# First modulation's second half in two quarters, and k blocks 4 to 7 of the first four tiles in two passes

## The chip, the cores and the metric

One NeuronCore of a Trainium2 chip runs the whole kernel as one program. The metric is the device time of one execution in microseconds; lower is better. The program drives five engines, each with its own instruction stream: TensorE (PE, with its weight loads as PEld), VectorE (DVE), ScalarE (ACT), GpSimd (POOL) and SyncE (SP), which here only issues DMAs. Streams meet through counting semaphores.

## The reference

A decoder layer on 512 tokens of width 1024, in float32: a token mixer, then a mixture of experts, then a final norm. The change lies in the very start, where the conditioning vector `c` is turned into a shift and a scale and applied to the normed input, and in the first columns of the input projection:

```python
mod = silu(c) @ w_ada + b_ada            # w_ada: 1024 x 6144
sh1, sc1, g1, sh2, sc2, g2 = split(mod, 6)
h = rmsnorm(x, norm_mix_g) * (1 + sc1) + sh1
proj = h @ w_in                          # w_in: 1024 x 7168
```

Only `sh1` and `sc1` (columns 0 to 1023 and 1024 to 2047 of `w_ada`) are needed for `h`. The kernel holds `h` transposed, channels on the partitions, as eight blocks `k` of 128 channels by 512 tokens.

## The kernel before

**Precision.** A float32 product is made of three matmuls: `h` and the weights are each split into a high part and the rest (`h_hi`, `h_lo`, `w_hi`, `w_lo`), and `mm3` (lines 571 to 573) issues hi by hi, hi by lo and lo by hi. One output tile (128 columns of `w_in` by 512 tokens) takes 8 blocks `k` of three matmuls, 24 in all.

**Weight chunks.** `w_in` comes in chunks of 256 columns (1 MB), two tiles each. SyncE loads chunk n into `w_raw[n % 2]`; ScalarE makes `w_hi` of it (`split_hi`, L952) and VectorE `w_lo` (`split_lo`, L1203). Both targets have two slots, so `split_hi(n)` waits until the last tile of chunk n-2 is done (`chunk_used`), and tile 2n may not start on TensorE until `split_lo(n)` has ended (`pe.wait_ge(s_lo, n + 1)`, L749). Chunks 0 and 1 are split in halves by k (`half_hi`, `half_lo`: blocks 0 to 3, then 4 to 7).

**Modulation.** The columns of `w_ada` come in eight pieces of 1 MB, two (k halves) for each of four groups `b` of 512 columns: b = 0 and 1 are the first 512 columns of shift and of scale, b = 2 and 3 their second 512. `ada_rows(b, h)` multiplies a piece with `silu(c)` (four small matmuls, each of which shows as two in the profile, so L585 x16 is both halves), `ada_out(b)` copies the sums out (ScalarE, L956), `ada_columns(b)` transposes them into columns (TensorE, L598). VectorE's `mod_columns(g)` then makes shift and scale of four blocks `k` at once: it waits for both groups of its half (`s_acp` at 2g + 2). After that `h_scale(k)` (VectorE, L1238), `h_high(k)` (ScalarE, L961) and `h_low(k)` (VectorE, L1244) make block k of `h`.

**The first four tiles** lie in four PSUM banks, since their first four blocks `k` are multiplied before the modulation of the other four is known. TensorE's order, written out by hand, is: blocks 0 to 3 of tiles 0 and 1; rows of b = 2; blocks 0 to 3 of tile 2; rows of b = 3 and columns of b = 2; blocks 0 to 3 of tile 3 with the columns of b = 3 inside; then blocks 4 to 7 of tiles 0 and 1, k by k in turn; then of tile 2; then of tile 3. From tile 4 on a loop over the steps runs tile after tile. On ScalarE the order after this is: copy out tiles 0 and 1 (L989), `split_hi(2)`, copy out tiles 2 and 3, `split_hi(3)`.

The order on SyncE is: the two halves of `x`, the pieces of b = 0 and 1, chunks 0 and 1, the pieces of b = 2 and 3, the masks, then chunk 2 once `w_lo` of chunk 0 is done.

Of the kernel before, what the change touches and what calls it, by code (L numbers as in the profile page):

```python
# [30 lines left out]
ALU = mybir.AluOpType  # L31
AX = mybir.AxisListType

P = 128
T = 512
D = 1024
KT = D // P
# [11 lines left out]
CHW = 256  # L49
# [16 lines left out]
C_C, C_BADA, C_GMIX, C_LB, C_ON = 0, 8, 24, 32, 40  # L66
# [27 lines left out]
def trunk_kernel(nc, xT, x, cols, consts, masks, w_ada, b_ada_row, w_in, w_o_hgrn, w_o_conv,  # L94
# [15 lines left out]
    with ctx:  # L110
# [10 lines left out]
        def at(name, where, shape, dt=F32, plus=0):  # L121
            return nc.alloc_sbuf_tensor_at(name, shape, dt, offset=placed[where] + plus)
# [27 lines left out]
        for l in range(1, NLEV + 1):  # L150
# [9 lines left out]
        ada_w = [at(f"ada_w{i}", r, [P, 4, T]) for i, r in  # L160
                 enumerate(("F", "K", "Q", "V", "TOT", "OG", "DG", "ST"))]
# [13 lines left out]
        cols_t = at("cols_t", "COLS", [P, C_ALL])  # L175
# [6 lines left out]
        mod1 = at("mod1", "SMALL", [P, 16])  # L182
# [13 lines left out]
        ada_s = at("ada_s", "SMALL", [P, 8], F32, 352)  # L196
# [27 lines left out]
        pp = ctx.enter_context(nc.psum_tensor("pp", [P, 1024], F32))  # L224
# [15 lines left out]
        s_ada = [sem(f"ada_piece{i}_loaded") for i in range(8)]  # L240
        s_raw = [sem(f"raw_chunk_loaded{i}") for i in range(2)]
        s_hi = sem("chunk_hi_done")
        s_lo = sem("chunk_lo_done")
# [13 lines left out]
        s_acp = sem("ada_columns_pe")  # L257
        s_md = sem("ada_columns_done")
# [4 lines left out]
        s_hl = sem("h_lo_done")  # L263
# [82 lines left out]
        s_as = sem("ada_columns_summed")  # L346
# [23 lines left out]
        def bank_of(s):  # L370
            return ha[:, s - 2, :] if s in (2, 3) else proj[:, s % 2, :]
# [71 lines left out]
        def chunk_view(ap, n):  # L443
            return ap[:, n % 2, :].rearrange("p (k n) -> p k n", k=4 if chunks[n][0] == "yb" else 8)
# [21 lines left out]
        def _(sp):  # L466
# [3 lines left out]
            wa = w_ada[0].rearrange("(k p) n -> p k n", p=P)  # L470

            def ada_first(b):
                for h in range(2):
                    i, c0 = 2 * b + h, D * (b % 2) + T * (b // 2)
                    sp.dma_start(ada_w[i][:, :, :], wa[:, 4 * h:4 * h + 4, c0:c0 + T]).then_inc(s_ada[i], 16)  # L475

            def chunk_load(n):
                sp.dma_start(chunk_view(w_raw, n), chunk_source(n)).then_inc(s_raw[n % 2], 16)
# [1 line left out]
            for h in range(2):  # L480
                sp.dma_start(xt_t[:, 4 * h:4 * h + 4, :], xTv[:, 4 * h:4 * h + 4, :]).then_inc(s_xt[h], 16)
            ada_first(0)
            ada_first(1)
            chunk_load(0)
            chunk_load(1)
# [82 lines left out]
        def _(pe):  # L568
            def mm3(outap, a_hi, a_lo, b_hi, b_lo, first, last):

                pe.matmul(outap, a_hi, b_hi, start=first, stop=False)  # L571
                pe.matmul(outap, a_hi, b_lo, start=False, stop=False)  # L572
                return pe.matmul(outap, a_lo, b_hi, start=False, stop=last)  # L573
# [6 lines left out]
            pe.wait_ge(s_par, 16 * 2)  # L580

            def ada_rows(b, h):
                pe.wait_ge(s_ada[2 * b + h], 16)
                for j in range(4):
                    mm = pe.matmul(ha[32 * j:32 * j + 32, b, :], cact32[:, 4 * h + j, :], ada_w[2 * b + h][:, j, :],  # L585
                                   start=(h == 0), stop=(h == 1))
                if h:
                    mm.then_inc(s_ao, 1)

            def ada_columns(b):  # L590
                pe.wait_ge(s_ac, b + 1)
                if b == 0:
                    pe.wait_ge(s_sq0, 1)
                elif b >= 2:
                    pe.wait_ge(s_md, 2)
                for c in range(4):
                    q = 512 * (b % 2) + P * c
                    mm = pe.transpose(pp[:, q:q + P], ada_r[:, b, P * c:P * c + P], ident)  # L598
                mm.then_inc(s_acp, 1)

            def first_part(s, k):
                n, t = steps[s][2], steps[s][3]
                hi, lo = chunk_view(w_hi, n), chunk_view(w_lo, n)
                mm = mm3(bank_of(s), hi[:, k, P * t:P * t + P], lo[:, k, P * t:P * t + P],
                         h_hi[:, k, :], h_lo[:, k, :], k == 0, k == KT - 1)
                if k == KT - 1:
                    mm.then_inc(s_tile, 1)
# [18 lines left out]
            pe.wait_ge(s_lf, 2)  # L626
            for k in range(4):
                first_part(2, k)
            ada_rows(3, 0)
            ada_rows(3, 1)  # L630
            ada_columns(2)
            for k in range(4):
                first_part(3, k)
                if k == 1:
                    ada_columns(3)
            pe.wait_ge(s_lo, 1)
            for k in range(4, KT):
                pe.wait_ge(s_hl, k + 1)
                first_part(0, k)
                first_part(1, k)  # L640
            pe.wait_ge(s_lo, 2)
            for s in (2, 3):
                for k in range(4, KT):
                    first_part(s, k)

            def level(qd, l):
# [283 lines left out]
        def raw_ready(eng, n):  # L930
            eng.wait_ge(s_raw[n % 2], 16 * (n // 2 + 1))

        @block.scalar
        def _(act):
# [19 lines left out]
            def ada_out(b):  # L954
                act.wait_ge(s_ao, b + 1)
                act.activation(ada_r[:, b, :], ha[:, b, :], ACT.Copy).then_inc(s_ac, 1)  # L956

            def h_high(k):
                act.wait_ge(s_md, 2 * (k // 4) + 2)
                act.wait_ge(s_ht, k + 1)  # L960
                act.activation(h_hi[:, k, :], xt_t[:, k, :], ACT.Identity, bias=mod1[:, k:k + 1]).then_inc(s_hh, 1)  # L961

            def half_hi(n, half):
                raw_ready(act, n)
                part_ = slice(1024 * half, 1024 * half + 1024)
                act.activation(w_hi[:, n, part_], w_raw[:, n, part_], ACT.Copy).then_inc(s_hi if half else s_hf, 1)
# [11 lines left out]
            half_hi(0, 1)  # L978
            half_hi(1, 1)
            ada_out(2)  # L980
            ada_out(3)
            for k in range(4, KT):
                h_high(k)

            def evacuate(s, kind, tile, n, t):
                bank = bank_of(s)
# [185 lines left out]
        def _(dve):  # L1172
# [47 lines left out]
            def mod_columns(g):  # L1220

                dve.wait_ge(s_acp, 2 * g + 2)
                dve.tensor_reduce(ada_s[:, :], pp[:, :].rearrange("p (q j r) -> p q j r", j=4, r=32)[:, :, :, 0], AX.X,
                                  ALU.add).then_inc(s_as, 1)
                dve.wait_ge(s_as, g + 1)
                dve.tensor_tensor(mod1[:, :].rearrange("p (a k) -> p a k", a=2)[:, :, 4 * g:4 * g + 4],
                                  ada_s[:, :].rearrange("p (a k) -> p a k", a=2),
                                  cols_t[:, C_BADA:C_BADA + 16].rearrange("p (a k) -> p a k", a=2)[:, :, 4 * g:4 * g + 4],
                                  ALU.add).then_inc(s_md, 1)
                dve.wait_ge(s_md, 2 * g + 1)  # L1230
                dve.scalar_tensor_tensor(mod1[:, 8 + 4 * g:12 + 4 * g], mod1[:, 8 + 4 * g:12 + 4 * g], 1.0,
                                         cols_t[:, C_GMIX + 4 * g:C_GMIX + 4 * g + 4],
                                         ALU.add, ALU.mult).then_inc(s_md, 1)

            def h_scale(k):
                dve.wait_ge(s_md, 2 * (k // 4) + 2)
                dve.wait_ge(s_rdone, 1)
                dve.scalar_tensor_tensor(xt_t[:, k, :], xt_t[:, k, :], mod1[:, 8 + k:9 + k], rst[:, :],  # L1238
                                         ALU.mult, ALU.mult).then_inc(s_ht, 1)

            def h_low(k):
                dve.wait_ge(s_ht, k + 1)
                dve.wait_ge(s_hh, k + 1)
                dve.scalar_tensor_tensor(h_lo[:, k, :], xt_t[:, k, :], mod1[:, k:k + 1], h_hi[:, k, :].bitcast(F32),  # L1244
                                         ALU.add, ALU.subtract).then_inc(s_hl, 1)

            def half_lo(n, half):
                dve.wait_ge(s_hi if half else s_hf, n + 1)
                raw_ready(dve, n)
                part_ = slice(1024 * half, 1024 * half + 1024)  # L1250
                dve.tensor_tensor(w_lo[:, n, part_], w_raw[:, n, part_], w_hi[:, n, part_].bitcast(F32),
                                  ALU.subtract).then_inc(s_lo if half else s_lf, 1)

            for g in range(2):
                mod_columns(g)
                h_scale(4 * g)
                if g == 0:
                    half_lo(0, 0)
                for k in range(4 * g + 1, 4 * g + 4):
                    h_scale(k)  # L1260
                    h_low(k - 1)
                h_low(4 * g + 3)
                if g == 0:
                    half_lo(1, 0)
                    half_lo(0, 1)
                    half_lo(1, 1)

            def evacuate(s, kind, tile, n, t):
                bank = bank_of(s)
# [487 lines left out]
            for tt in range(TT + 1):  # L1757
# [7 lines left out]
                if tt:  # L1765
                    q = tt - 1
# [154 lines left out]
```

## Time and profile before

| what | value |
|---|---|
| median of 3 runs | 866.62 us (866.6, 866.62, 869.02) |
| the profiled execution's own time | 867.63 us |
| its span, first to last instruction | 865.8 us |
| mean granted TensorE clock | 0.984 |
| PE, DVE, ACT busy | 93%, 55%, 24% of the span |
| instructions | 14136 |

Times in the trace count from the span's start. A row of the timeline gives start and duration in microseconds, engine, line, operation, output and inputs; a bracket gives the idle time of that engine before it and who ended it. The ends of matmuls are modelled, so successive matmuls overlap in the rows: the step from one start to the next is the rate. The granted clock is the share of full speed (2.4 GHz) that TensorE was given: 1.00 or 0.50 (1.2 GHz).

### The profile page before, as it was taken

How to read it: one execution, taken by the hardware profiler on the slowest of the kernel's cores; microseconds unless marked ns; L12 is line 12 of the kernel's file. 1: busy time of each engine (PE TensorE's matmuls, PEld its weight loads, DVE VectorE, ACT ScalarE, POOL GpSimd, SP SyncE). 2: the span in 40 equal slices, each digit the busy share in tenths (PEclk: the TensorE clock that was granted, in tenths of full speed). 3: DMA queues.
4: the chain of work that ended last, by engine and by line, in shares of the span. 5: the costliest groups of instructions: out<-in, count | busy, mean ns of one | idle time of the engine just before them, and what ended most of it. 6: DMA issues, size and time to landing. Idle time of an engine off the chain costs nothing.

```text
span 865.8 us, 14136 instructions
## 1 busy us (share of the span) xinstructions
PE 805.5 (93%) x5706; PEld 585.9 (68%) x5706; DVE 476.3 (55%) x644; ACT 205.0 (24%) x263; POOL 143.5 (17%) x199
## 2 busy tenths in 40 slices
PE   2899999999999999999999999989999999999960
PEld 0578889888789887778888898655555555555520
DVE  2648999996799964878777465611111111111117
ACT  3441221222331126522222423100000000000012
POOL 0000231221413200320000000012222222222220
PEclk9999999999999999999999999999999999999995
DMA  9923231313131311278774949997999999998316
GB/s 311 370 81 103 98 98 50 98 50 97 50 98 51 98 49 49 98 246 280 240 241 160 341 142 388 401 381 289 378 395 395 400 390 400 394 396 303 125 43 274
DMA packets 102207, 191.59 MB, mean 221 GB/s; under 512 B 4151, under 2 KB 41287, under 8 KB 102161
## 3 DMA queue, kind: packets, MB, share of 16 engines
q1 hardware_dynamic: 89042, 160.79, 51.4%
q10 hardware_dynamic: 9168, 19.40, 6.6%
q0 software_dynamic: 3952, 10.76, 3.4%
q8 instruction: 33, 0.54, 0.3%
q14 instruction: 12, 0.10, 0.0%
HBM read 182.54 MB, written 10.49 MB: 223 GB/s over the span
## 4 chain that ended last, share of the span: by engine, by line
PE 82%; DVE 9%; DMA 3%; issue 2%; SPq 1%; ACT 1%; POOL 1%; DVEq 0%; POOLq 0%; ACTq 0%
PE proj L869 19%; PE proj L571 14%; PE proj L573 14%; PE proj L572 14%; PE ha L905 10%; PE pp L678 2%; DMA w_raw<-in_w_in 2%; PE pp L859 2%; DVE acc L1366 1%; SPq L475 1%; PE ha L891 1%; PE ha L708 1%; PE ha L741 1%; DVE rt L1540 1%; PE ha L711 1%
## 5 line engine op out<-in xcount | busy, mean ns | idle before, releaser
L869 PE MATMUL proj<-ew,heT 128*64 128x256 f32 x1536 | 175.0, 381 | 0.7 <-ACT heT L1142 0.7
L869 PEld LDWEIGHTS proj<-ew,heT 128*64 128x64 f32 x1536 | 107.9, 137 | 66.2 <-issue 16.4
L571 PE MATMUL proj<-h_hi,w_hi 128*128 128x512 f32 x368 | 146.8, 399 | 3.8 <-DVE h_lo L1244 3.2
L573 PE MATMUL proj<-h_hi,w_lo 128*128 128x512 f32 x368 | 144.1, 392 | 0.0
L572 PE MATMUL proj<-h_lo,w_hi 128*128 128x512 f32 x368 | 143.9, 391 | 0.0
L1203 DVE TENSOR_TENSOR w_lo<-w_raw,w_hi 128x2048 fp32r<-128x2048 f32 x36 | 82.4, 2289 | 20.4 <-ACT w_hi L952 20.3
L1366 DVE SCALAR_TENSOR_TENSOR acc<-u_t,cols_t,acc 128x512 f32<-128x512 f32 x120 | 91.1, 807 | 0.6
L905 PE MATMUL ha<-ew,aT 128*64 128x512 f32 x384 | 87.7, 598 | 0.9 <-DVE aT L1732 0.9
L571 PEld LDWEIGHTS proj<-h_hi,w_hi 128*128 128x128 f32 x368 | 69.5, 189 | 21.9 <-issue 7.6
L952 ACT ACTIVATE w_hi<-w_raw 128x2048 fp32r<-128x2048 f32 x36 | 68.7, 1908 | 65.8 <-PE proj L573 43.1
L572 PEld LDWEIGHTS proj<-h_lo,w_hi 128*128 128x128 f32 x368 | 69.6, 189 | 14.4 <-issue 0.5
L573 PEld LDWEIGHTS proj<-h_hi,w_lo 128*128 128x128 f32 x368 | 69.4, 189 | 14.7
L1737 DVE TENSOR_TENSOR y_sb<-ha,rows 128x512 f32<-128x512 f32 x24 | 16.6, 691 | 90.9 <-PE ha L905 90.9
L1831 POOL COPY gi<-idx_g 128x1 int32 (+1 forms) x25 | 4.7, 188 | 318.4 <-DVE idx_g L1715 185.2
L905 PEld LDWEIGHTS ha<-ew,aT 128*64 128x64 f32 x384 | 25.5, 136 | 46.1 <-issue 45.8
L1726 DVE TENSOR_TENSOR a_t<-proj,sg_t 128x256 f32<-128x256 f32 x24 | 10.2, 426 | 77.7 <-PE proj L869 77.7
L1732 DVE COPY aT<-ha 128x256 f32<-128x256 f32 x24 | 10.2, 425 | 74.0 <-PE ha L891 74.0
L1482 DVE SCALAR_TENSOR_TENSOR ada_acc<-ada_p,cact,ada_acc 128x512 f32<-128x512 f32 x64 | 47.9, 751 | 3.0 <-DMA ada_p<-in_w_ada 1.1
L1136 ACT ACTIVATE sg_t<-proj 128x256 f32<-128x256 f32 x24 | 9.2, 383 | 150.3 <-PE proj L869 150.3
L1142 ACT ACTIVATE heT<-pp 128x512 f32<-128x512 f32 x25 | 14.9, 597 | 102.1 <-PE pp L859 102.1
L571 PE MATMUL proj<-w_hi,m_hi 128*128 128x256 f32 x128 | 37.0, 289 | 0.0
L571 PE MATMUL proj<-w_hi,h_hi 128*128 128x256 f32 x128 | 36.8, 288 | 0.0
(254 smaller groups left out, 1211.7 us busy)
## 6 DMA issues: line engine op xcount, KB each, us to landing
ew<-in_w_gate SPq DMA_DIRECT2D x32, 1024.0 KB, 13.8
ew<-in_w_up SPq DMA_DIRECT2D x32, 1024.0 KB, 15.1
ew<-in_w_down SPq DMA_DIRECT2D x32, 1024.0 KB, 14.4
w_raw<-in_w_in SPq DMA_DIRECT2D x28, 1024.0 KB, 5.2
ada_p<-in_w_ada ACTq DMA_DIRECT2D x16, 1024.0 KB, 5.3
ada_w<-in_w_ada SPq DMA_DIRECT2D x8, 1024.0 KB, 13.8
w_raw<-in_w_o_hgrn SPq DMA_DIRECT2D x4, 1024.0 KB, 6.0
w_raw<-in_w_out SPq DMA_DIRECT2D x4, 1024.0 KB, 10.0
```

Of the source, the lines that this page charges most:

```text
L571: pe.matmul(outap, a_hi, b_hi, start=first, stop=False)
L572: pe.matmul(outap, a_hi, b_lo, start=False, stop=False)
L573: return pe.matmul(outap, a_lo, b_hi, start=False, stop=last)
L678: mm = pe.matmul(pp[64 * j:64 * j + keys, 32 * u:32 * u + 32], k_t[:, h, t0:t0 + keys], tblk(q_t[:, h, t0:t0 + 64], m, 1), start=True, sto ...
L859: mm = pe.transpose(pp[:, P * c:P * c + P], xg[:, P * c:P * c + P], ident)
L869: mm = pe.matmul(out_ps[JS * i:JS * i + JS, 0:FG], heT[:, c_, JS * j_:JS * j_ + JS], w[:, k, FG * i:FG * i + FG], start=(kb == 0), stop=(k ...
L905: mm = pe.matmul(ha[JS * i:JS * i + JS, 1, 0:DG_], aT[:, c_, JS * i_:JS * i_ + JS], w[:, k, DG_ * i:DG_ * i + DG_], start=(fb == 0), stop= ...
L952: act.activation(w_hi[:, n % 2, :], w_raw[:, n % 2, :], ACT.Copy).then_inc(s_hi, 1)
L1203: dve.tensor_tensor(w_lo[:, n % 2, :], w_raw[:, n % 2, :], w_hi[:, n % 2, :].bitcast(F32), ALU.subtract).then_inc(s_lo, 1)
L1366: dve.scalar_tensor_tensor(acc[:, ct, :], src, tap, acc[:, ct, :], ALU.mult, ALU.add).then_inc(s_cv, 1)
L1482: dve.scalar_tensor_tensor(dst, ada_p[g % 2][:, k, :], cact[:, kk:kk + 1], dst, ALU.mult, ALU.add).then_inc(s_aa, 1)
L1737: dve.tensor_tensor(y_sb[:, :], ha[:, 1, 0:DG_], rows[:, 3, 0:DG_], ALU.mult).then_inc(s_y, 1)
```

## The change

The pieces of b = 2 and 3 are cut another way. Each now holds 256 columns of shift and the 256 columns of scale that belong to the same two blocks: b = 2 is the modulation of blocks 4 and 5, b = 3 that of blocks 6 and 7. Each piece comes in two DMAs of 512 KB with rows of 1 KB, where it was one DMA of 1 MB with rows of 2 KB. VectorE computes each quarter by itself (`mod_quarter`) as soon as its one group of columns is there. TensorE's order becomes: rows of b = 2; tile 2's blocks 0 to 3 with the columns of b = 2 after block 1; tile 3's; rows of b = 3; blocks 4 and 5 of tile 0; columns of b = 3; blocks 4 and 5 of tile 1, 2, 3; then blocks 6 and 7 of tiles 0, 1, 2, 3. ScalarE makes `h_hi` of blocks 4 and 5 before it copies out the rows of b = 3.

```diff
--- before.py
+++ after.py
@@ -471,8 +471,13 @@
 
             def ada_first(b):
                 for h in range(2):
-                    i, c0 = 2 * b + h, D * (b % 2) + T * (b // 2)
-                    sp.dma_start(ada_w[i][:, :, :], wa[:, 4 * h:4 * h + 4, c0:c0 + T]).then_inc(s_ada[i], 16)
+                    i, ks = 2 * b + h, slice(4 * h, 4 * h + 4)
+                    if b < 2:
+                        sp.dma_start(ada_w[i][:, :, :], wa[:, ks, D * b:D * b + T]).then_inc(s_ada[i], 16)
+                    else:
+                        for a in range(2):
+                            sp.dma_start(ada_w[i][:, :, CHW * a:CHW * a + CHW],
+                                         wa[:, ks, D * a + CHW * b:D * a + CHW * b + CHW]).then_inc(s_ada[i], 16)
 
             def chunk_load(n):
                 sp.dma_start(chunk_view(w_raw, n), chunk_source(n)).then_inc(s_raw[n % 2], 16)
@@ -580,7 +585,7 @@
             pe.wait_ge(s_par, 16 * 2)
 
             def ada_rows(b, h):
-                pe.wait_ge(s_ada[2 * b + h], 16)
+                pe.wait_ge(s_ada[2 * b + h], 32 if b >= 2 else 16)
                 for j in range(4):
                     mm = pe.matmul(ha[32 * j:32 * j + 32, b, :], cact32[:, 4 * h + j, :], ada_w[2 * b + h][:, j, :],
                                    start=(h == 0), stop=(h == 1))
@@ -626,21 +631,26 @@
             pe.wait_ge(s_lf, 2)
             for k in range(4):
                 first_part(2, k)
+                if k == 1:
+                    ada_columns(2)
+            for k in range(4):
+                first_part(3, k)
             ada_rows(3, 0)
             ada_rows(3, 1)
-            ada_columns(2)
-            for k in range(4):
-                first_part(3, k)
-                if k == 1:
+            pe.wait_ge(s_lo, 1)
+            for s in (0, 1):
+                for k in (4, 5):
+                    pe.wait_ge(s_hl, k + 1)
+                    first_part(s, k)
+                if s == 0:
                     ada_columns(3)
-            pe.wait_ge(s_lo, 1)
-            for k in range(4, KT):
-                pe.wait_ge(s_hl, k + 1)
-                first_part(0, k)
-                first_part(1, k)
             pe.wait_ge(s_lo, 2)
             for s in (2, 3):
-                for k in range(4, KT):
+                for k in (4, 5):
+                    first_part(s, k)
+            for s in range(4):
+                for k in (6, 7):
+                    pe.wait_ge(s_hl, k + 1)
                     first_part(s, k)
 
             def level(qd, l):
@@ -956,7 +966,7 @@
                 act.activation(ada_r[:, b, :], ha[:, b, :], ACT.Copy).then_inc(s_ac, 1)
 
             def h_high(k):
-                act.wait_ge(s_md, 2 * (k // 4) + 2)
+                act.wait_ge(s_md, (2, 2, 4, 6)[k // 2])
                 act.wait_ge(s_ht, k + 1)
                 act.activation(h_hi[:, k, :], xt_t[:, k, :], ACT.Identity, bias=mod1[:, k:k + 1]).then_inc(s_hh, 1)
 
@@ -978,9 +988,11 @@
             half_hi(0, 1)
             half_hi(1, 1)
             ada_out(2)
+            h_high(4)
+            h_high(5)
             ada_out(3)
-            for k in range(4, KT):
-                h_high(k)
+            h_high(6)
+            h_high(7)
 
             def evacuate(s, kind, tile, n, t):
                 bank = bank_of(s)
@@ -1233,7 +1245,7 @@
                                          ALU.add, ALU.mult).then_inc(s_md, 1)
 
             def h_scale(k):
-                dve.wait_ge(s_md, 2 * (k // 4) + 2)
+                dve.wait_ge(s_md, (2, 2, 4, 6)[k // 2])
                 dve.wait_ge(s_rdone, 1)
                 dve.scalar_tensor_tensor(xt_t[:, k, :], xt_t[:, k, :], mod1[:, 8 + k:9 + k], rst[:, :],
                                          ALU.mult, ALU.mult).then_inc(s_ht, 1)
@@ -1251,19 +1263,38 @@
                 dve.tensor_tensor(w_lo[:, n, part_], w_raw[:, n, part_], w_hi[:, n, part_].bitcast(F32),
                                   ALU.subtract).then_inc(s_lo if half else s_lf, 1)
 
-            for g in range(2):
-                mod_columns(g)
-                h_scale(4 * g)
-                if g == 0:
-                    half_lo(0, 0)
-                for k in range(4 * g + 1, 4 * g + 4):
-                    h_scale(k)
-                    h_low(k - 1)
-                h_low(4 * g + 3)
-                if g == 0:
-                    half_lo(1, 0)
-                    half_lo(0, 1)
-                    half_lo(1, 1)
+            def mod_quarter(b):
+
+                ks = slice(2 * b, 2 * b + 2)
+                dve.wait_ge(s_acp, b + 1)
+                dve.tensor_reduce(ada_s[:, 0:4], pp[:, 512 * (b % 2):512 * (b % 2) + 512].rearrange("p (q j r) -> p q j r", j=4, r=32)[:, :, :, 0],
+                                  AX.X, ALU.add).then_inc(s_as, 1)
+                dve.wait_ge(s_as, b)
+                dve.tensor_tensor(mod1[:, :].rearrange("p (a k) -> p a k", a=2)[:, :, ks],
+                                  ada_s[:, 0:4].rearrange("p (a k) -> p a k", a=2),
+                                  cols_t[:, C_BADA:C_BADA + 16].rearrange("p (a k) -> p a k", a=2)[:, :, ks],
+                                  ALU.add).then_inc(s_md, 1)
+                dve.wait_ge(s_md, 2 * b - 1)
+                dve.scalar_tensor_tensor(mod1[:, 8 + 2 * b:10 + 2 * b], mod1[:, 8 + 2 * b:10 + 2 * b], 1.0,
+                                         cols_t[:, C_GMIX + 2 * b:C_GMIX + 2 * b + 2],
+                                         ALU.add, ALU.mult).then_inc(s_md, 1)
+
+            mod_columns(0)
+            h_scale(0)
+            half_lo(0, 0)
+            for k in range(1, 4):
+                h_scale(k)
+                h_low(k - 1)
+            h_low(3)
+            half_lo(1, 0)
+            half_lo(0, 1)
+            half_lo(1, 1)
+            for b in (2, 3):
+                mod_quarter(b)
+                h_scale(2 * b)
+                h_scale(2 * b + 1)
+                h_low(2 * b)
+                h_low(2 * b + 1)
 
             def evacuate(s, kind, tile, n, t):
                 bank = bank_of(s)
```

## Rows read from the trace of the kernel before

**Rows 1.** The page: busy time by engine, and the chain that ended last, by engine.

```profile
PE 805.5 (93%) x5706; PEld 585.9 (68%) x5706; DVE 476.3 (55%) x644; ACT 205.0 (24%) x263; POOL 143.5 (17%) x199
...
PE 82%; DVE 9%; DMA 3%; issue 2%; SPq 1%; ACT 1%; POOL 1%; DVEq 0%; POOLq 0%; ACTq 0%
```

**Rows 2.** Timeline of TensorE, 38 to 61.4 and 373 us (start, duration, operation, idle).

```profile
38.17 0.50 PE L571 MATMUL ha<-h_hi,w_hi 128*128 128x512 f32 x1
...
46.50 0.40 PE L573 MATMUL ha<-h_hi,w_lo 128*128 128x512 f32 x1
...
48.73 0.47 PE L571 MATMUL proj<-h_hi,w_hi 128*128 128x512 f32 x1 [1.84 <-DVE h_lo L1244]
...
55.66 0.39 PE L573 MATMUL proj<-h_hi,w_lo 128*128 128x512 f32 x1
55.89 0.39 PE L571 MATMUL ha<-h_hi,w_hi 128*128 128x512 f32 x1
...
61.33 0.39 PE L571 MATMUL proj<-h_hi,w_hi 128*128 128x512 f32 x1
...
372.91 0.50 PE L571 MATMUL proj<-cs_hi,w_hi 128*128 128x512 f32 x1 [1.72 <-DVE mb L1309]
```

**Rows 3.** Windows: busy time and count by engine, granted clock, DMA share, GB/s.

```profile
46.90:48.70 1.80, 0.00 (x0) 0.00 (x0) 1.54 (x4) 1.39 (x2) 0.00 (x0) 1.00 0.03 9
50.50:52.30 1.80, 1.80 (x6) 1.33 (x5) 1.49 (x3) 0.72 (x1) 0.00 (x0) 0.50 0.00 0
360.00:380.00 20.00, 16.24 (x69) 12.48 (x68) 15.27 (x20) 4.31 (x6) 11.33 (x5) 1.00 0.41 134
```

**Rows 4.** Timeline, the small matmuls and copies of the second half's modulation.

```profile
36.32 1.92 PE L585 MATMUL ha<-ada_w,cact 128*32 128x512 f32 x16
...
41.16 1.92 PE L585 MATMUL ha<-ada_w,cact 128*32 128x512 f32 x16
...
43.15 0.60 ACT L956 ACTIVATE ada_r<-ha 128x512 f32<-128x512 f32 x1 [4.24 <-PE ha L585]
...
44.90 0.60 PE L598 MATMUL pp<-con_t,ada_r 128*128 128x128 f32 x4
```

**Rows 5.** Timeline of VectorE and ScalarE from the modulation to `h_lo` of block 4.

```profile
45.54 0.19 DVE L1223 TENSOR_REDUCE ada_s<-pp 128x8 f32<-128x32 f32 x1 [7.69 <-PE pp L598]
...
46.16 1.42 DVE L1238 SCALAR_TENSOR_TENSOR xt_t<-xt_t,mod,rst 128x512 f32<-128x512 f32 x2
...
47.83 0.75 DVE L1244 SCALAR_TENSOR_TENSOR h_lo<-xt_t,mod,h_hi 128x512 fp32r<-128x512 f32 x1 [0.26 <-ACT h_hi L961]
```

**Rows 6.** Timeline of the split of weight chunk 2, after tiles 0 and 1.

```profile
55.41 1.28 ACT L989 ACTIVATE acc<-proj 128x512 f32<-128x512 f32 x2 [4.02 <-PE proj L573]
...
56.58 1.91 ACT L952 ACTIVATE w_hi<-w_raw 128x2048 fp32r<-128x2048 f32 x1
...
58.52 2.29 DVE L1203 TENSOR_TENSOR w_lo<-w_raw,w_hi 128x2048 fp32r<-128x2048 f32 x1 [6.28 <-ACT w_hi L952]
```

**Rows 7.** Windows: 24 to 26 us moves rows of 1 KB, 32 to 34 rows of 2 KB.

```profile
24.00:26.00 2.00, 1.28 (x11) 0.37 (x11) 0.72 (x1) 0.60 (x1) 0.00 (x0) 1.00 1.10 348
32.00:34.00 2.00, 2.00 (x11) 1.66 (x10) 1.74 (x3) 1.40 (x3) 0.00 (x0) 1.00 1.06 389
```

**Rows 8.** SyncE's DMA issues by timeline, and by the DMA view their landing.

```profile
20.54 3.53 SPq L475 DMA_DIRECT2D ada_w<-in_w_ada  x1
...
24.11 2.93 SPq L475 DMA_DIRECT2D ada_w<-in_w_ada  x2
27.08 1.81 SPq L475 DMA_DIRECT2D ada_w<-in_w_ada  x1
...
ada_w<-in_w_ada SPq DMA_DIRECT2D x2, 1024.0 KB, 11.6
ada_w<-in_w_ada SPq DMA_DIRECT2D x1, 1024.0 KB, 14.6
...
w_raw<-in_w_in SPq DMA_DIRECT2D x2, 1024.0 KB, 9.4
```

## The prediction

> **What bounds the kernel now.** I read the page first: TensorE is busy 93% of the span and 82% of the chain that ended last is TensorE's [rows 1]. So a change that moves no TensorE work can gain only where TensorE stands still or runs at the lower clock. I then listed TensorE's idle times in the timeline. Between the first projection matmul and 107 us there is one: after the matmul at 46.50 nothing runs until 48.73, 1.84 us by the bracket, ended by `h_lo` [rows 2]. This is the wait for the second half's modulation. The windows show a second loss beside it: through the gap the granted clock is 1.00, and from 50.5 to 52.3 it is 0.50 [rows 3], the lower level of 1.2 GHz. It fell just after TensorE had stood still. Its price: the 24 matmuls of tiles 0 and 1 from 48.73 to 55.89 took 7.16 us, the 24 of tiles 2 and 3 from 55.89 to 61.33 took 5.44 us, a pitch of 0.227 [rows 2]. So the fall cost 1.72 us. Together the wait and the fall are worth 3.7 us at most: the step from 46.50 to 48.73 is 2.23, less a pitch 2.0, plus 1.7.
>
> Third, because the wait lies ahead of a fixed piece of work, I asked what limits the next thing, tile 4 at 61.33. It needs `w_lo` of weight chunk 2, whose target slot is free only when tile 1 is done. The rows give that chain [rows 2, 6]: tile 1's last matmul at 55.66 ends at 56.05; ScalarE copies out tile 1 (its two copies run 55.41 to 56.69), then makes `w_hi` 56.58 to 58.49; VectorE makes `w_lo` 58.52 to 60.81. From 56.05 to 60.81 is 4.76 us. TensorE started tile 4 at 61.33 without a wait, so the slack is about 0.4 us, and only because tiles 2 and 3 put 24 matmuls, 5.4 us, behind tile 1.
>
> **The change part by part.** *The wait in front of blocks 4 to 7.* TensorE's work up to the last pass is unchanged in count: 24 matmuls, the rows of b = 3 and two sets of columns lie between 38.17 and 46.73 (the start at 46.50 plus a pitch), 8.56 us [rows 2]. The new order puts between them 24 more, blocks 4 and 5 of all four tiles, 5.45 us. If nothing waits, the last pass (blocks 6, 7) starts at 38.17 + 8.56 + 5.45 = 52.18.
>
> Does anything wait? Blocks 4, 5: tile 2's first six matmuls end at 38.17 + 1.4 = 39.6, the columns take 0.6 [rows 4], `h_lo` of block 4 ended 48.58 - 44.90 = 3.7 us after the columns began and block 5's about 0.7 later [rows 4, 5]. So they are ready at about 43.3 and 44.0. TensorE wants them after tiles 2 and 3 (5.45), the columns (0.4) and the rows of b = 3 (1.9): 38.17 + 7.8 = 46.0. Slack 2 us. Blocks 6, 7: rows of b = 3 end at about 46.0, their copy takes 0.6 and starts 2.0 after the rows began [rows 4], so it is out at 46.7, before block 5 of tile 0 is through (46.0 + 1.4 = 47.4). The columns start there; 3.7 us later, and here a little more since both scales go before the first `h_low` (0.7 at most, which is one of them), block 6 is ready at 51.1 to 51.8 against 52.18, and block 7 0.7 later against its use 0.7 later. No wait; the slack is only 0.4 to 1.1. So this wait goes: 2.0 us, and the fall of the clock at this place with it.
>
> *VectorE and SyncE.* `mod_quarter` twice instead of `mod_columns` once adds three small operations, 0.6 us by their steps from 45.54 to 46.16 [rows 5]. They lie in VectorE's idle time (7.69 us ahead of 45.54), so nothing. Uncovered they would cost 0.6. SyncE issues four more DMAs. A bound from below is nothing, since SyncE's next work waits for `w_lo` of chunk 0; from above 4 x 3.5, the longest issue of a piece [rows 8]: the pieces would be issued by 28.9 + 14 = 42.9, the masks and chunk 2 (36.7 before) by about 46, and chunk 2, which took 9.4 to land, would be there at 55, when `w_hi` first needs it (below). I take nothing: half of each piece is half an issue, and the slack is 9 us.
>
> *Rows of 1 KB.* Where the weight chunks' 1 KB rows move, the rate is 348 GB/s, against 389 with the pieces' 2 KB rows [rows 7]: 3.01 against 2.70 us for 1 MB. The first pair of pieces, issued at 20.54 and 24.11 with 11.6 us in the median, lands at about 32.6 and 35.3; with 0.3 us more each the second lands at 35.9. TensorE wants it at 36.32 [rows 4]: covered, by 0.4. The last piece, issued at 27.08 plus 14.6 = 41.7, lands at about 42.9, and is wanted at 44.1 now, since tile 3 goes first. So nothing, with 0 and 2.4 as ends: 2.4 if the second piece takes the slowest landing of its kind, 14.6 instead of about 11.2, and lands at 38.7. I take nothing, since the rate's own rows put it at 35.9. The Trainium skill, DMA: Bandwidth & Descriptors, section Specifications, has 512 B as the least size for line rate, so by it the 1 KB rows would cost nothing; the 348 against 389 of this trace do not agree, and the measured pair decides. The same page (Bandwidth, Measured) asks for transfers of at least 1 MiB, and the change halves them; that is the fourth rival's direction.
>
> *What is late next.* Tile 1 now ends after the first 12 matmuls of the last pass: its last matmul starts at 52.18 + 12 x 0.227 - 0.23 = 54.68, ends at 55.07, and 4.76 us later, at 59.83, `w_lo` of chunk 2 is done. From the end of `h_lo` (47.83 + 0.75) to the matmul it released was 0.15 [rows 2, 5], so tile 4 starts at 59.98. Behind tile 1 there are only the 12 matmuls of tiles 2 and 3: they are through at 52.18 + 24 x 0.227 = 57.63. So TensorE waits from 57.8 (end of the last) to 59.98, 2.2 us, in a place where it did not wait before. Queued behind it on TensorE is everything: tile 4 and the whole projection. Tile 4 moves from 61.33 to 59.98: -1.35 us.
>
> *The clock again.* The new gap is longer than the one that goes. What idle time lets the clock fall here is bounded by rows: 1.84 us was followed by a fall [rows 2, 3]; 1.72 us before 372.91 was not, since all of 360 to 380 has 1.00 [rows 2, 3]. 2.2 us is beyond both, so I take a fall, at the measured 1.72. Ends: 0 and 1.72. Then tile 4's work is through as if it had started at 61.70: +0.37 against the profiled execution.
>
> **The sum, and against what.** Profiled: wait -2.0, clock there -1.7, new wait +2.3 (59.98 - 57.63), clock here +1.7: +0.3 to +0.4. From 867.63 that is 868.0. The median of the runs is 866.62, 1.0 below the profiled execution; I do not know whether the clock fell in those runs too. If it falls in both or in neither, the difference is the same +0.35, since without a fall the kernel before starts tile 4 at 61.33 - 1.72 = 59.61. I put the forecast on the median: 867.0. Behind tile 4 TensorE's chain runs on without a large wait, so a shift is carried to the end as it is. About 0.3% (2.6 us) is what a measurement of this kernel tells from no change.
>
> **The rivals.** (1) *The clock holds in the new gap* while it fell at the old one. For it: the 1.7 us that kept the clock. Against: 2.2 is more than 1.84. Time: 866.62 - 1.35 = 865.3. (2) *Slower: the clock falls in the new gap, and in the runs of before it did not at the old one.* It is decided by where the limit lies, between 1.72 and 1.84 us of standing still by the rows, so the old gap is right at it and the new one past it; that the median lies 1.0 us below the profiled execution, where it did fall, speaks for it, that a profile may cost time by itself against. Time: 59.98 + 1.72 - 59.61 = +2.1, 868.7. (3) *The whole 3.7 comes home*, the split of chunk 2 being hidden anyway. It would need `split_hi(2)` ahead of tile 1's end, which `chunk_used` forbids, or a copy and split chain of 2.5 us where the rows have 4.76. Time: 862.9. (4) *The halved transfers land late* and the second piece holds TensorE at 36.3. It decides once 2 MB after 29.9 (35.3 less two times 2.70) need more than 6.4 us, below 328 GB/s, where the rows have 348. Price up to 2.4; with half of that on top of the forecast, 868.2.
>
> **How the numbers follow.** Forecast 45%, (1) 23%, (2) 17%, (3) 8%, (4) 7%. The range 864.7 to 868.8 holds the forecast and (1), (2), (4) but for their edges, and leaves (3) out. The likeliest case by itself is 866.5 to 867.6. Faster by more than 0.3% (below 864.0) is (3) and an edge of (1): 11%. Slower by more than 0.3% (above 869.2) is (2) and (4) coming together or running over: 9%. Within: 80%.
>
> **What would show it.** The wait ahead of tile 0's block 4 is gone, and blocks 6, 7 start near 52.2 with no idle before them. A new idle time of about 2.2 us stands before tile 4's first matmul, ended by `w_lo` L1203, whose own wait is for `w_hi` L952. The windows after it show a granted clock under 1.00 (forecast, 2) or 1.00 (1). `ada_rows` of b = 2 still starts near 36.3; if later, (4). I am wrong if tile 4 starts without a wait, if a wait for `h_lo` remains in front of block 6, or if a part of the shift at tile 4 is not found at the end.

## The result, and the profile after

The changed kernel takes 870.03 us in the median of 14 runs (867.38 to 872.39), the kernel before 867.31 in 14 runs beside it (866.06 to 871.18). The ratio is 1.0027, 95% interval 1.0015 to 1.0040: slower by 0.3%. A second comparison on another occasion (e8 below) gave 1.0014, 0.9998 to 1.0029. The forecast was 867.0 in 864.7 to 868.8, so the measured time lies outside the range, above it. The profiled execution took 870.24, its span 868.4. Two executions in the later comparisons, one of e5 (1052 us) and one of the kernel before beside it (4633 us), were disturbed and are left out of the numbers.

The page has the same engines busy as before [rows 1]; TensorE's busy time is 2.5 us longer with the same 5706 matmuls, which is a first sign of a lower clock rather than of more work:

```profile
PE 808.0 (93%) x5706; PEld 586.6 (68%) x5706; DVE 476.7 (55%) x647; ACT 204.9 (24%) x263; POOL 143.3 (17%) x199
```

The timeline of the stretch from block 4 to tile 4, to be read against [rows 2, 5, 6]:

```profile
46.73 0.50 PE L576 MATMUL proj<-h_hi,w_hi 128*128 128x512 f32 x1
...
52.79 0.39 PE L576 MATMUL proj<-h_hi,w_hi 128*128 128x512 f32 x1
...
55.28 0.39 PE L578 MATMUL proj<-h_hi,w_lo 128*128 128x512 f32 x1
...
55.70 0.60 ACT L1001 ACTIVATE acc<-proj 128x512 f32<-128x512 f32 x1 [0.76 <-PE proj L578]
...
56.20 1.91 ACT L962 ACTIVATE w_hi<-w_raw 128x2048 fp32r<-128x2048 f32 x1
...
58.14 2.29 DVE L1215 TENSOR_TENSOR w_lo<-w_raw,w_hi 128x2048 fp32r<-128x2048 f32 x1 [5.26 <-ACT w_hi L962]
...
60.49 0.50 PE L576 MATMUL proj<-h_hi,w_hi 128*128 128x512 f32 x1 [2.10 <-DVE w_lo L1215]
```

No idle time stands before blocks 4 (46.73) and 6 (52.79). The last pass starts 21.58 us after the first projection matmul (31.21), where the forecast had 52.18 - 30.70 = 21.48; the wait went as forecast. In its place TensorE stands still for 2.10 us ahead of tile 4, ended by `w_lo` of chunk 2: the chain of [rows 6], 4.76 us from the end of tile 1 to the end of `w_lo`, is unchanged (55.67 to 60.43), and there are only 12 matmuls to cover it. The rows of b = 2 start at 36.86, 5.65 us after the first projection matmul, against 5.62 before, so the halved transfers held nothing up. The windows show what came after this gap, and a second place of the same kind (busy time by engine, granted clock, DMA share, GB/s):

```profile
61.60:64.80 3.20, 3.20 (x9) 2.52 (x8) 1.60 (x1) 0.00 (x0) 0.00 (x0) 0.50 0.98 314
...
566.70:570.00 3.30, 3.01 (x14) 1.71 (x16) 0.00 (x0) 0.24 (x1) 1.12 (x2) 0.50 1.04 377
```

The third column from the right is the granted clock. It fell to 0.50 (1.2 GHz) behind tile 4's gap, and again at 566 us, just behind TensorE's wait for the second gather of tokens for the experts:

```profile
565.65 0.66 PE L869 MATMUL pp<-con_t,xg 128*128 128x128 f32 x4 [2.08 <-DMA xg<-h_rows,gi]
```

In the profile before, that gather had an idle time of 1.80 us and no fall.

The two profiled executions can be compared stretch by stretch. In the one before, a group of small matmuls of the token mixer (L678) and the last group of matmuls of the kernel start at

```profile
257.51 2.06 PE L678 MATMUL pp<-q_t,k_t 128*64 128x32 f32 x64 [0.74 <-DVE st L1377]
...
834.19 3.65 PE L905 MATMUL ha<-ew,aT 128*64 128x512 f32 x16 [0.93 <-DVE aT L1732]
```

and in the one after at

```profile
258.37 2.06 PE L688 MATMUL pp<-q_t,k_t 128*64 128x32 f32 x64 [0.73 <-DVE st L1408]
...
836.83 3.65 PE L915 MATMUL ha<-ew,aT 128*64 128x512 f32 x16 [0.93 <-DVE aT L1763]
```

The first projection matmul starts 0.51 us later (31.21 against 30.70). From there to the first of these rows the change costs 0.35 us (227.16 against 226.81), the forecast's number, with a fall of the clock in each. The later stretch costs 1.78 us more than before (578.46 against 576.68), and it is the one with the gather: its tokens are there 0.29 us later, counted from the group before them, and the fall behind it takes the rest, 1.5 us. The three add up to the 2.6 us between the spans.

**A tool for what follows.** Each run is recorded with its mean granted clock. Each of the 14 profiles has one fall at the very end, when TensorE has finished. In the eight that have no other, the mean is 0.985 to 0.987; in the four with one more it is 0.983 or 0.984, in the two with two more 0.981 or 0.982. One fall costs 1.7 us of 866, or 0.002; so 0.984 or less is read as at least one fall while TensorE still had work. The fall at the end starts between 838 and 843 us, which by itself moves the mean by as much as 0.002, so 0.985 does not exclude a fall, and the mean does not say where one was. By this reading all 14 runs of the changed kernel have at least one.

### The profile page after: what moved, and what is told of

It is laid out like the page before. It is cut to its first block, busy times and chain, and to the rows that moved or that the text cites. A ratio compares the mean times of both kernels' runs of the same rounds, so it can differ in the third digit from the quotient of the medians.

```text
span 868.4 us, 14143 instructions
## 1 busy us (share of the span) xinstructions
PE 808.0 (93%) x5706; PEld 586.6 (68%) x5706; DVE 476.7 (55%) x647; ACT 204.9 (24%) x263; POOL 143.3 (17%) x199
## 4 chain that ended last, share of the span: by engine, by line
PE 83%; DVE 9%; DMA 3%; issue 2%; ACT 2%; POOL 1%; SPq 0%; POOLq 0%; DVEq 0%; ACTq 0%
PE proj L879 19%; PE proj L576 14%; PE proj L578 14%; PE proj L577 14%; PE ha L915 10%; PE pp L688 2%; PE pp L869 2%; DVE acc L1397 1%; DMA xt_t<-in_xT 1%; PE ha L901 1%; PE ha L590 1%; PE ha L718 1%; PE ha L751 1%; DVE w_lo L1215 1%; DVE rt L1571 1%
```

## The experiments

Theory after the result: the work is as forecast and the loss is the clock, which falls more often in the new gap than in the old one. Rivals: the 1 KB loads delay the start; the new order costs time by itself; the 2.7 us are chance.

**e1.** TensorE is kept running through the new gap, with matmuls whose result nobody reads.

```diff
+                if s == 4:
+                    busy(ha[:, 3, :], 8)
                 if t == 0:
                     pe.wait_ge(s_lo, n + 1)
```

> The changed kernel with 8 throw-away 128x128 matmuls in the idle time ahead of tile 4 (2.10 us idle in its profile, one such matmul takes 0.24 us). Clock theory: what the change loses is the fall of the clock in that gap; with TensorE kept running the clock stays at 1.00 there, tile 4 still starts near 60.5, and the time is 1.7 us below the changed kernel's 870.0, so about 868.3, within 0.1% of the kernel before. Rival, the 1 KB loads or the new order itself: the clock is held but the time stays near 870.

867.94 us (12 runs), ratio to the kernel before 0.9998 (0.9981 to 1.0015). Tile 4 starts where it did in the timeline, and the clock is whole behind it:

```profile
60.48 0.50 PE L576 MATMUL proj<-h_hi,w_hi 128*128 128x512 f32 x1 [0.32 <-DVE w_lo L1217]
```

and in the windows (busy time by engine, granted clock, DMA share, GB/s):

```profile
61.00:65.00 4.00, 4.00 (x19) 3.28 (x19) 2.19 (x1) 0.00 (x0) 0.00 (x0) 1.00 0.86 280
```

Eight matmuls that do nothing take about 2 us off the changed kernel's time (its ratios are 1.0027 and, in e8, 1.0014, measured on other occasions), though tile 4 starts no earlier. So the rivals, which have the loss elsewhere, fall for the larger part. In 7 of the 12 runs the mean clock is still 0.984 or less.

**e2.** The same in the kernel before, ahead of block 4: `busy(ha[:, 3, :], 7)`.

> The kernel before with 7 throw-away 128x128 matmuls in its 1.84 us wait ahead of tile 0's block 4. Clock theory: if the clock fell there in all runs, the time drops by 1.7 us to about 865.6; if in only some of them, by that part of 1.7 (half: 866.5); if only in the profiled one, by nothing. The profile shows 1.00 all through the first 110 us. Rival (the fall is no cost, TensorE has slack behind it): no change in time though the clock holds.

868.32 us, ratio 0.9996 (0.9980 to 1.0013). A miss: no gain. The gap is filled (block 4 at 48.46, idle 0.28) and the clock whole behind it (1.00 from 49 to 53 us), but in 8 of 12 runs the mean clock is still 0.984 or less, against 18 of the 35 runs of the unfilled kernel beside them, and the one profile says where:

```profile
563.64 0.55 PE L860 MATMUL pp<-con_t,xg 128*128 128x128 f32 x3 [2.79 <-DMA xg<-h_rows,gi]
```

and in the windows (busy time by engine, granted clock, DMA share, GB/s):

```profile
565.80:569.00 3.20, 3.20 (x18) 1.84 (x17) 0.00 (x0) 0.00 (x0) 0.30 (x1) 0.54 1.04 388
```

The gather is a second place where the clock may fall, in either kernel, and has to be filled too before small differences can be read. What is missing in this group of twelve is the top: of 35 runs of the kernel before beside it, 12 lay at 869.7 to 871.6; of these twelve none lies above 869.6.

**e3.** The kernel before with the last four pieces in two DMAs each, rows of 1 KB; nothing else.

```diff
-                    sp.dma_start(ada_w[i][:, :, :], wa[:, 4 * h:4 * h + 4, c0:c0 + T]).then_inc(s_ada[i], 16)
+                    for a in range(2 if b >= 2 else 1):
+                        w = CHW if b >= 2 else T
+                        sp.dma_start(ada_w[i][:, :, w * a:w * a + w],
+                                     wa[:, 4 * h:4 * h + 4, c0 + w * a:c0 + w * a + w]).then_inc(s_ada[i], 16)
```

> The kernel before with only the cut of its last four modulation pieces into two DMAs each with rows of 1 KB; order and modulation as before. Clock theory: no difference (ratio 1.000 within 0.1%), TensorE's rows of group 2 still start near 36.3; the last piece, needed at 41.2 here and already just in time, lands up to 1.2 us later, so up to 1.2 us more wait is possible at 41 that the changed kernel does not have. Rival, late data: rows of group 2 start later than 36.5 and the time is 1 to 2 us longer.

867.86 us, ratio 1.0004 (0.9986 to 1.0022). The rate is 348 GB/s from 34 to 38 us, while the pieces move (386 there before), as forecast from [rows 7], and both sets of rows start when they did, 4.84 us apart as in [rows 4]:

```profile
36.40 1.92 PE L588 MATMUL ha<-ada_w,cact 128*32 128x512 f32 x16
41.24 1.92 PE L588 MATMUL ha<-ada_w,cact 128*32 128x512 f32 x16
```

and in the windows (busy time by engine, granted clock, DMA share, GB/s):

```profile
34.00:38.00 4.00, 4.00 (x27) 2.11 (x26) 3.76 (x4) 2.25 (x3) 0.00 (x0) 1.00 1.10 348
```

The interval of the time alone would leave room for 1.9 us; it is the rows, here and in the changed kernel (36.86), that put the late-data rival (4) of the prediction out.

**e4.** The chain itself is shortened: chunk 2 is split by halves of k, and tile 4 waits for the first half of `w_lo` only.

```diff
+                if s == 2:                       # ScalarE
+                    chunk_used(act, 0)
+                    half_hi(2, 0)
+                    half_hi(2, 1)
...
+                if s == 2:                       # VectorE
+                    half_lo(2, 0)
+                    half_lo(2, 1)
...
+                if s == 4:                       # TensorE; for block 4: s_lo at 3
+                    pe.wait_ge(s_lf, 3)
```

> The changed kernel with weight chunk 2 split into hi and lo by halves of k, so that tile 4 needs only the first half. Theory (the chain tile 1, copy, w_hi, w_lo is what holds tile 4): the chain shortens from 4.2 us of splitting to 2.3, tile 4 starts at 58.7 instead of 60.5 with an idle time of about 0.3 us, the clock holds; the time is 1.8 + 1.7 = 3.5 us below 870.0, so 866.5. Rival (something else holds tile 4): it starts at 60.5 as before.

867.19 us, ratio 0.9991 (0.9974 to 1.0007), 2.5 us below e8's changed kernel where 3.5 was expected of 870.0. Tile 4 starts 2 us earlier, as expected, so the chain was what held it:

```profile
58.50 0.47 PE L576 MATMUL proj<-h_hi,w_hi 128*128 128x512 f32 x1 [0.44 <-ACT acc L1005]
```

The rest of the expected gain is most likely at the gather: 11 of the 12 runs have a mean clock of 0.984 or less, and the profile has its only fall there (0.50 from 563 to 566 us, after 1.74 us idle).

**e5, e6, e7.** Both places are filled: `busy(ha[:, 3, :], 7)` ahead of the first `tokens(j + 1)`, in the kernel before (e5, with e2's edit), in the changed one (e6, with e1's) and in e4's (e7, whose gap is too short to need it).

> The kernel before with throw-away matmuls in both places where TensorE stands still for about 2 us: 7 ahead of tile 0's block 4 and 7 ahead of the second gather of tokens for the experts (idle 1.80 us at 564.5, after which the clock fell in some profiles). Clock theory: the spread of the runs, 865.6 to 871.6 for the kernel before, shrinks to about 1.5 us, around 866.3, and the granted clock of all runs is about 0.986. Rival (the spread comes from the DMAs): the spread stays.

> The changed kernel with 8 throw-away matmuls ahead of tile 4 and 7 at the experts' second gather. With no fall of the clock left in either, it stands against the filled kernel before for the change without its clock. Theory: tile 4 starts at 59.98 against 59.61, so +0.35 us, about 866.7. Rival (the change has a cost besides the clock, as later first modulation by its loads): +1 us or more, 867.5.

> The changed kernel with chunk 2 split by halves of k and 7 throw-away matmuls at the experts' second gather. Theory: tile 4 starts at 58.5, 1.1 us ahead of the filled kernel before (59.6 without a fall) and the gap is 0.4 us, so 865.2, a ratio of 0.998 to the kernel before or less. Rival (something behind tile 4 takes the gain back): 866.3 as the filled kernel before.

Measured: e5 866.39 in eleven runs, ratio 0.9977 (0.9961 to 0.9994); e6 866.87, ratio 0.9986 (0.9970 to 1.0001); e7 865.83, ratio 0.9973 (0.9956 to 0.9990). The runs of e5 lie within 865.8 and 867.4, with clocks of 0.985 or more. The kernel before spans 865.7 to 872.1 beside them, with clocks down to 0.980. So its spread is mostly falls of the clock. e7 lies 0.6 us below e5 where 1.1 was expected, and their intervals overlap. Tile 4 of e5 starts at 59.65 (forecast for the kernel before without a fall: 59.61).

With the falls filled away in both, the change costs 866.87 - 866.39 = 0.5 us, near the +0.35 of the prediction (0.8 us by the two ratios). The intervals of the ratios overlap, so the times show only that it is small. The profiles have it more closely: from the first projection matmul to the same small matmuls of the token mixer it is 225.63 us in e6 and 225.19 in e5, both without a fall, so +0.44.

**e8.** The changed kernel again, beside e5 to e7.

> The changed kernel as it is, beside the others on one chip. Clock theory: nearly all runs have a fall ahead of tile 4, so the time lies about 2 us above its own filled version and about 2.5 us above the kernel before, granted clock 0.980 to 0.984. Rival (the 2.7 us of the first comparison were chance): within 1 us of the kernel before.

869.66 us in 12 runs, ratio 1.0014; 2.8 us above its filled version e6. All its clocks are 0.981 to 0.984: not one run without a fall, whereas 13 of 34 runs of the kernel before beside it lie below 867.1, with 0.985 or more. Its profile fell in both places again. With the first comparison that is 26 of 26 runs of the changed kernel with at least one fall, against 54 of 104 of the kernel before in the three groups whose clocks are recorded. The kernel before has a median of 867.71 in this group and 866.39 when filled (e5): filling is worth 1.3 us there and 2.8 in the changed kernel. By the means of the same runs it is 1.7 and 2.2, so the size of the difference is not settled.

**e9, e10.** Only the gather is filled, so that what is left of the spread belongs to the gap ahead of tile 4 (e9) or ahead of block 4 (e10).

> The changed kernel with 7 throw-away matmuls at the experts' second gather alone: the gap ahead of tile 4 keeps its fall. Clock theory: 1.7 us above the kernel filled in both places (866.9), so 868.6, with granted clocks near 0.984 in all runs, none at 0.986. Rival (the fall ahead of tile 4 happens in some runs only): two groups of runs, 866.9 and 868.6.

> The kernel before with 7 throw-away matmuls at the experts' second gather alone: the wait ahead of block 4 keeps its chance of a fall. Clock theory: two groups of runs, 866.4 without a fall (0.986) and 868.1 or more with one (0.984), the first the larger, since 23 of 35 runs of the kernel before lay below 867.8. Rival (it falls in every run, as ahead of tile 4): all near 868.1.

e9: 868.73 us, ratio 1.0011 (0.9997 to 1.0025); 10 of 12 runs at 0.984 or less. e10: 867.40 us, ratio 1.0004 (0.9989 to 1.0020); 6 of 12. So the fall is a matter of chance in both places. The longer gap had it more often, but 10 against 6 of 12 can be chance by itself. The profiles of both happened to be executions without a fall, the timeline of e9 first,

```profile
60.88 0.50 PE L576 MATMUL proj<-h_hi,w_hi 128*128 128x512 f32 x1 [2.10 <-DVE w_lo L1217]
```

and in the windows (busy time by engine, granted clock, DMA share, GB/s):

```profile
61.00:65.00 4.00, 4.00 (x18) 3.30 (x19) 2.29 (x1) 0.27 (x1) 0.00 (x0) 1.00 0.78 240
```

The same two views of e10, the gap ahead of block 4:

```profile
48.84 0.47 PE L571 MATMUL proj<-h_hi,w_hi 128*128 128x512 f32 x1 [1.84 <-DVE h_lo L1246]
```

and in the windows (busy time by engine, granted clock, DMA share, GB/s):

```profile
49.00:53.00 4.00, 4.00 (x18) 3.29 (x18) 3.09 (x5) 1.45 (x2) 0.00 (x0) 1.00 0.01 2
```

The same 2.10 and 1.84 us were followed by a fall in the profiles of the two kernels themselves. Against the versions filled in both places, the medians are 868.73 - 866.87 = 1.9 us higher in the changed kernel and 867.40 - 866.39 = 1.0 us in the one before. These pairs were measured on two occasions, between which the unfilled kernel before itself moved from 867.71 to 867.23; by the ratios to it the two steps are 0.0025 and 0.0027, so no difference between them is shown. In the kernel before, filling one place alone gained nothing (e2 0.9996, e10 1.0004), filling both did (e5 0.9977); why is open.

**e11, a version that beats both.** e7 with tile 2's copy-out between the halves of `w_hi`, since that copy ended e7's last 0.44 us.

```diff
                     half_hi(2, 0)
+                    evacuate(s, kind, tile, n, t)
                     half_hi(2, 1)
+                    continue
```

> As the kernel with halves and 7 throw-away matmuls at the gather, and ScalarE copies tile 2 out between the two halves of w_hi. The 0.44 us idle time ahead of tile 4 was ended by that copy; theory: it is gone, tile 4 starts at 58.1, and the time is 0.3 to 0.4 us less, 865.5. Rival (the second half of w_lo now comes late for block 4 of tile 4): a wait inside tile 4 and no gain.

864.99 us, ratio 0.9968 (0.9952 to 0.9983): the fastest kernel of the study, 2.2 us below the kernel before beside it, part of which is the filling (e5). Tile 4 starts at 58.13 with an idle time of 0.18 us, as expected. That it is faster than e7 (0.9973) is not shown, since the intervals overlap.

**e12.** No filling ahead of tile 4, only another order: blocks 4 and 5 of tile 3 go to the end.

```diff
-            for s in (2, 3):
-                for k in (4, 5):
-                    first_part(s, k)
-            for s in range(4):
-                for k in (6, 7):
+            for k in (4, 5):
+                first_part(2, k)
+            for s in range(4):
+                for k in (6, 7) if s < 3 else range(4, KT):
```

> The changed kernel with 7 throw-away matmuls at the gather and, in place of filling, another order: blocks 4 and 5 of tile 3 move from the first pass to the end, next to its blocks 6 and 7. Nothing is added or removed. Theory: TensorE waits 0.9 us ahead of block 6 and 0.8 ahead of tile 4, in place of 2.1 in one piece; neither brings a fall; tile 4 starts 0.3 earlier, so 2.0 us below the same kernel in the first order (868.6), 866.6. Rival (the sum of idle time decides, not the longest piece): the clock falls all the same and the time stays at 868.3.

867.10 us, ratio 0.9993 (0.9976 to 1.0009), 1.6 us below e9, which differs only in the order. Two short waits stand for the long one, 10 of 12 runs have 0.985 or more, and the profile is whole:

```profile
52.19 0.50 PE L576 MATMUL proj<-h_hi,w_hi 128*128 128x512 f32 x1 [0.64 <-DVE h_lo L1257]
...
60.06 0.50 PE L576 MATMUL proj<-h_hi,w_hi 128*128 128x512 f32 x1 [0.74 <-DVE w_lo L1216]
```

and in the windows (busy time by engine, granted clock, DMA share, GB/s):

```profile
51.00:60.00 9.00, 7.68 (x33) 5.64 (x31) 3.83 (x4) 5.07 (x8) 0.00 (x0) 1.00 0.00 0
```

TensorE stood still for 1.4 us in all, and seldom paid for it: 2 of 12 runs at 0.984 or less against 10 of 12 in e9, on the same occasion. This pair shows most plainly that the one long wait brings the falls and the time.

## Why the prediction was wrong

*What held.* The wait ahead of block 4 went and none came ahead of block 6, with some 0.6 us to spare there (an estimate: VectorE's two `h_lo` of blocks 6 and 7 start at 51.47 and take 1.41 together), inside the 0.4 to 1.1 of the prediction. The next bound was named rightly, with its chain of 4.76 us and its place; the new gap was forecast at 2.2 us and measured 2.10. The step from the first projection matmul (30.70 before, 31.21 after) to tile 4 shrank from 30.63 to 29.28 us: 1.35, the forecast number; and as the clock fell behind both gaps in the two profiles, that stretch cost +0.35. SyncE's four issues and the 1 KB rows cost nothing that can be seen (e3), and the three small operations held up no matmul in the profile. Without falls the change costs +0.44 in the profiles and 0.5 in the medians against +0.35 (e5, e6).

*The step that failed* is in the sum: "If it falls in both or in neither, the difference is the same +0.35". It was true where it applied, but the forecast was put on it with 45%, as if the clock's fate were one and the same for both kernels. I had read one fall in one profiled execution, taken 1.72 and 1.84 us of standing still as the two sides of a limit, and so concluded that both gaps were past it. The runs show no such limit: 1.84 and 2.10 us were each followed by a fall in one execution and by none in another (e10, e9), and at the gather 1.74 us (e4) and 1.79 us (e8) were followed by a fall while 1.80 us in the profile before was not. What differs is how often it happens: at least one fall in 26 of 26 runs of the changed kernel and in 54 of 104 of the kernel before. Filling both places takes 2.8 us off the one and 1.3 off the other (e8 to e6, the kernel before to e5). Rival (2), given 17% at 868.7, had the right direction, but its all or nothing was wrong as well, and its time falls short of the measured 870.0.

*A second step that failed* is "Behind tile 4 TensorE's chain runs on without a large wait, so a shift is carried to the end as it is". The profile before has an idle time of 1.80 us ahead of the gather at 564 us, longer than the 1.72 that the prediction took for one side of its limit. It is of the same kind as the gap ahead of tile 4, and I passed over it since the clock had held there. Between the two profiles this stretch cost 1.8 us. The clock falls there in either kernel (profiles of the changed kernel, e8, e4 and e2). In 7 of 12 runs of e1 and 8 of 12 of e2 it fell somewhere although the first gap was filled; that this was the gather is argued from those profiles. What filling it gains by itself is not settled: e8 to e9 is 0.9 us by the medians of two occasions and 0.3 by the ratios, and in the kernel before, from 867.23 to 867.40 on one occasion, nothing.

*The account.* The forecast of 867.0 stood on a median of 866.62 from three runs; beside the changed kernel the same kernel had 867.31, so 0.7 of the 3.0 us between forecast and measurement is the base. The rest is the difference of the two kernels. Between the profiles: 0.5 (later start of the projection), 0.35 (the change's own stretch), 1.8 (the gather and the fall behind it) make the 2.6 us. Between the medians of e8 and its kernel before, 1.9 us: 0.5 is the change without falls (e6 less e5), the other 1.5 are falls, 2.8 less 1.3, with the reservation on its size given at e8. That falls are the larger part of the loss is shown by e6 against e8 and by e12 against e9. How the loss divides between the gap ahead of tile 4 and the gather is not shown, and why the gather should fall more often in the changed kernel, if it does, is open. Two more things stay open. The projection's first matmul started at 30.4 to 30.8 us in the five profiles of kernels with the old order and at 30.7 to 31.8 in the nine with the new one, about 0.5 us later in the mean. The small matmuls from 20.5 us on are slower there too (the row that takes 2.58 us in the profile before takes 3.53 in the one after); nothing in the change lies ahead of it, and five against nine profiles don't tell chance from cause. And in several kernels one or two runs of twelve lie 3 us above the others with a clock of 0.982 to 0.984, and nearly a third of the runs of the kernel before (31 of 104) lie at 869 to 872, nearly all with 0.980 to 0.982, more than its one profiled fall explains; no profile shows such a run.

## What to carry to other kernels

In this kernel a wait on TensorE of about 2 us has two prices: its length, and 1.7 us times the chance that the clock falls behind it. Before moving work over such a wait, follow the next chain with a fixed length (here copy, `w_hi`, `w_lo`) to see whether the wait goes or only moves; here a wait that moved and grew by 0.3 us made the kernel 0.3% slower, though tile 4 itself came 1.35 us sooner after the start of the projection. List every wait of that length, also those behind which the clock happened to hold. Where it can't be shortened, split it in two or fill it, and judge such changes by many runs and their mean clock, since one profile shows one draw.

## What the hardware showed unexpectedly

The granted clock after the same idle time is not the same from execution to execution: after 2.10 us ahead of tile 4 it was 0.50 in the profiles of the changed kernel and of e8, and 1.00 in that of e9. With the gather filled, 10 of 12 runs with the 2.10 us gap and 6 of 12 with the 1.84 us gap had at least one fall. It did not fall in any of the 14 profiles after the 1.7 us at 370 to 374 us, but it did in two after 1.74 and 1.79 us at the gather (e4, e8), where TensorE waits another 0.69 us a moment later. The gather itself is uneven as well: from the first group of gathered tokens to the second TensorE took 10.97 us (e4) to 12.44 (e5), and e5 had no fall there. A kernel whose work doesn't vary spreads over 6 us (865.7 to 872.1) mostly by such falls, and over 1.6 us with the two places filled (e5).
